# Gate and up weights of the next expert issued ahead of the down weights of the current one

## The chip, the cores and the metric

The kernel runs on one core of a Trainium2 chip. The metric is the device time of one execution in microseconds (us). Before the change it is 1476.72 us, the median of three runs (1476.27 to 1479.73 us).

## The reference, cut to what matters

One layer of a streaming encoder for 1024 prompt rows and 128 sample rows of width 1024: attention and a gated linear recurrence, an output projection, and then a mixture of 16 experts. Each row goes to two experts of one group of four. The change is in the expert stage only:

```python
for e in range(N_EXPERTS):                       # 16
    u = silu(hf @ w_e_gate[e]) * (hf @ w_e_up[e])      # 1024 -> 512
    y = y + gates[:, e:e+1] * (u @ w_e_down[e])        # 512 -> 1024
```

All values are float32. The weights of an expert are a gate, an up and a down matrix of 2 MB each.

## The kernel before, in words

The stages before the experts (conditioning, projection, mixing, output projection, routing) are not touched. The routing stage sorts the routed rows into lists of up to 128 rows that all go to the same expert, the lists of expert 0 first. The profiled execution has 27 lists (L2085 runs once for each). The routing stage also issues the loads of experts 0 and 1, before the lists are known (L1622, L1623).

The expert stage (`experts`, from L1758) walks through the lists. A matrix product in float32 is made of three in a shorter format: each operand is split in a high part (a copy by ScalarE, ACT) and the rest (a subtraction by VectorE, DVE). The weights lie in two slots by the expert's parity: `w_gu` (gate and up) and `w_dn` (down). The rest replaces the loaded weights in place. The high part of gate and up, `w_h`, has a single buffer; that of down, `w_dh`, has two.

In the step of list t, TensorE (PE) runs `hidden(t)` (48 matmuls, L1942 to L1944), `turn_x(t+1)` (8 transposes, L1927), `down(t-1)` (24 matmuls, L1958 to L1960) and `turn_u(t)` (4 transposes, L1966). So the first record of L1927 in a step marks the end of a list's hidden matmuls.

When list t is the last of its expert, ACT and DVE split the next expert's weights in this step. The order on ACT is fixed by the program: silu of list t, `keep_x(t+1)`, eight copies of gate and up (L1996), `keep_u(t)`, a wait for the down weights (L1999, L2000), four copies of them (L2006); only then comes the silu of list t+1 (L2026). DVE follows with the rests: L2085, L2048, L2055, then L2043 (the gated result of list t-1), L2081 and L2062. `hidden(t+2)` on PE waits for `u_ready` and `xl_ready`, which DVE sets with L2085 and L2048 of the next step.

The SyncE queue (SP) issues the weight loads of experts 2 to 15. For expert e it waits until the hidden matmuls of expert e-2 are done (`gu_mm`), issues gate and up (L346), waits until the down matmuls of expert e-2 are done (`dn_mm`), and issues down (L349). Then it goes on to expert e+1. The queue is in order, so a wait of one expert holds back the loads of the next. GpSimd (POOL) issues three indirect transfers for each list on its own queue: the gather of the rows (L1861), the gather of the output gates (L1866), and the addition of the finished rows to the output in memory (L1889), which waits for DVE's L2043.

Of the kernel before, what the change touches and what calls it, by code (L numbers as in the profile page):

```python
# [50 lines left out]
NE = 16  # L51
# [7 lines left out]
LISTS = 2 * NT + NE - 1  # L59
SLOTS = LISTS + 2  # L60
# [36 lines left out]
def one(t):  # L97
    return slice(t, t + 1) if isinstance(t, int) else bass.ds(t, 1)
# [239 lines left out]
    sp.dma_start(b["w_r"][:, :, :], d["w_router"].rearrange("(k p) n -> p k n", p=P)).then_inc(b["w_r_loaded"], 16)  # L338


def load_expert(sp, b, d, e, par, after_gu=None, after_dn=None):

    if after_gu:
        sp.wait_ge(*after_gu)
    for j, w in enumerate((d["w_gate"], d["w_up"])):
        sp.dma_start(b["w_gu"][:, par, j, :, :], w[one(e), :, :].rearrange("a (k p) n -> p (a k) n", p=P)).then_inc(b["gu_loaded"][par], 16)  # L346
    if after_dn:
        sp.wait_ge(*after_dn)
    sp.dma_start(b["w_dn"][:, par, :, :], d["w_down"][one(e), :, :].rearrange("a (k p) n -> p (a k) n", p=P)).then_inc(b["dn_loaded"][par], 16)  # L349

OUT_A, OUT_B, M0, M1, M2, M3, PJ0, PJ1 = range(8)
# [1214 lines left out]
def route(nc, b, d, router_bias):  # L1568
# [3 lines left out]
    with ExitStack() as ctx:  # L1572
# [3 lines left out]
        def sem(name):  # L1576
            return ctx.enter_context(nc.semaphore("q_" + name))
# [35 lines left out]
        s = {n: sem(n) for n in names}  # L1613
        block = ctx.enter_context(nc.Block())

        @block.sync
        def _(sp):
            sp.dma_start(bias[:, :], router_bias.partition_broadcast(P)).then_inc(s["bias_loaded"], 16)

            sp.sem_inc(b["gu_loaded"][1], 1)  # L1620
            sp.sem_inc(b["dn_loaded"][1], 1)
            for e in range(2):  # L1622
                load_expert(sp, b, d, e, e)  # L1623

        @block.gpsimd
        def _(pool):
# [131 lines left out]
def experts(nc, b, d):  # L1758
# [10 lines left out]
    with ExitStack() as ctx:  # L1769
# [3 lines left out]
        def sem(name):  # L1773
            return ctx.enter_context(nc.semaphore("e_" + name))
# [21 lines left out]
        s = {n: sem(n) for n in names}  # L1796
# [17 lines left out]
        def after(base, t):  # L1814
            return slice(base + t, base + t + 1) if isinstance(t, int) else bass.ds(t + base, 1)
# [16 lines left out]

        @block.sync
        def _(sp):
            def load(e, par):

                done = sp.value_load(b["list_info"][0:1, bass.ds(e + (SLOTS - 2), 1)], min_val=0, max_val=LISTS)
                load_expert(sp, b, d, e, par, (s["gu_mm"], done + 1), (s["dn_mm"], done + 1))

            with sp.Fori(1, NE // 2) as i:  # L1840
                load(i * 2, 0)
                load(i * 2 + 1, 1)
            for par in range(2):
                sp.wait_ge(gu_loaded[par], NE * 16 + par)
                sp.wait_ge(dn_loaded[par], NE // 2 * 16 + par)
# [290 lines left out]
```

## Time and profile before

| | |
|---|---|
| median of three runs | 1476.72 us |
| profiled execution | 1478.23 us |
| span of its trace | 1476.5 us |
| PE busy | 1276.9 us (86% of the span) |
| DVE busy | 771.5 us (52%) |
| ACT busy | 545.0 us (37%) |
| weight loads by L346 and L349 | 48 of 2048 KB |

The page cuts the span into 40 slices of 36.9 us. In the last fifteen, the expert stage, PE is mostly at nine tenths, and the DMA engines' share reads 7 to 9 tenths in most:

```profile
PE   5529999999999999994969973699999999969964
PEclk7759999999999999995779995799999999989988
DMA  9970000000000000005273328458667979898874
```

Each digit is the busy share of a slice in tenths; PEclk is the clock granted to TensorE, in tenths of full speed. Where PE reads 6 late in the span, PE has stood still.

### The profile page before, as it was taken

The numbers are of one execution on the slowest core, as the hardware profiler recorded it, in microseconds if no ns is written. First come the engines' busy times: TensorE is split into PE (matmuls) and PEld (weight loads), VectorE is DVE, ScalarE is ACT, GpSimd is POOL, SyncE is SP. The second block draws the span as 40 slices with busy tenths as digits, with TensorE's granted clock in tenths as the row PEclk, the third lists the DMA queues.
The fourth block names the chain that finished last, engine by engine and source line by source line (L and its number), as shares of the span: only waits on it lengthen the run. The fifth ranks groups of instructions, "written<-read, shape, count | busy, mean of one in ns | idle before, by whom it ended". The sixth has DMA issues, their size and how long they took to land. (4 is left out here: it accounts for less than half of the span.)

```text
span 1476.5 us, 21409 instructions
## 1 busy us (share of the span) xinstructions
PE 1276.9 (86%) x6661; PEld 919.6 (62%) x6662; DVE 771.5 (52%) x1187; ACT 545.0 (37%) x916; POOL 264.5 (18%) x287
## 2 busy tenths in 40 slices
PE   5529999999999999994969973699999999969964
PEld 0014666665766666564648863588888787858853
DVE  0010656466475655647244446555528665865752
ACT  0011535435253443524143330444416444644540
POOL 1000101102010110204000000233133233323313
PEclk7759999999999999995779995799999999989988
DMA  9970000000000000005273328458667979898874
GB/s 355 415 286 11 5 15 0 14 0 14 14 0 14 0 14 0 14 2 130 38 202 124 118 100 291 151 182 273 215 184 250 332 256 309 300 309 253 266 281 85
DMA packets 87921, 215.01 MB, mean 146 GB/s; under 512 B 16577, under 2 KB 20289, under 8 KB 84818
## 3 DMA queue, kind: packets, MB, share of 16 engines
q1 hardware_dynamic: 75794, 170.58, 32.3%
q0 software_dynamic: 12096, 44.05, 11.4%
q8 instruction: 16, 0.26, 0.1%
q14 instruction: 15, 0.12, 0.0%
HBM read 188.31 MB, written 26.23 MB: 145 GB/s over the span
## 5 line engine op out<-in xcount | busy, mean ns | idle before, releaser
L481 PE MATMUL psum<-w_in_sb,x_res 128*128 128x512 f32 (+1 forms) x864 | 353.2, 563 | 4.4 <-DVE x_res L471 4.4
L481 PEld LDWEIGHTS psum<-w_in_sb,x_res 128*128 128x128 f32 x864 | 160.9, 191 | 164.1 <-issue 156.8
L1942 PE MATMUL psum<-e_w_h,e_x_h 128*128 128x512 f32 x432 | 174.9, 405 | 29.5 <-DVE w_gu L2055 23.1
L1943 PE MATMUL psum<-w_gu,e_x_h 128*128 x432 | 171.8, 398 | 0.0
L1944 PE MATMUL psum<-e_w_h,e_x_l 128*128 128x512 f32 x432 | 171.6, 397 | 0.0
L2055 DVE TENSOR_TENSOR w_gu<-w_gu,e_w_h 128x1024 f32 x128 | 146.7, 1220 | 20.5 <-ACT e_w_h L1996 20.5
L1996 ACT ACTIVATE e_w_h<-w_gu 128x1024 fp32r x128 | 123.0, 1048 | 53.9 <-issue 33.0
L1889 POOL DMA_INDIRECT out<-e_work,e_to x26 | 87.6, 3371 | 302.3 <-DVE e_work L2043 302.3
L1942 PEld LDWEIGHTS psum<-e_w_h,e_x_h 128*128 128x128 f32 x432 | 83.4, 193 | 47.9 <-DVE w_gu L2055 23.6
L1944 PEld LDWEIGHTS psum<-e_w_h,e_x_l 128*128 128x128 f32 x432 | 83.3, 193 | 18.2
L1943 PEld LDWEIGHTS psum<-w_gu,e_x_h 128*128 128x128 f32 x432 | 83.4, 193 | 17.0
L1958 PE MATMUL psum<-e_w_dh,e_u_h 128*128 x216 | 86.5, 400 | 2.1 <-DVE e_u_l L2081 2.1
L1960 PE MATMUL psum<-e_w_dh,e_u_l 128*128 x216 | 84.4, 391 | 0.0
L1959 PE MATMUL psum<-w_dn,e_u_h 128*128 x216 | 84.2, 390 | 0.0
L2085 DVE TENSOR_TENSOR e_work<-e_work,psum 128x512 f32<-128x512 f32 x27 | 18.6, 687 | 125.2 <-ACT e_work L2026 123.1
L2062 DVE TENSOR_TENSOR w_dn<-w_dn,e_w_dh x64 | 74.0, 1222 | 18.9 <-ACT e_w_dh L2006 18.9
L2026 ACT ACTIVATE e_work<-psum 128x512 f32<-128x512 f32 x27 | 16.1, 597 | 173.8 <-PE psum L1944 173.8
L2006 ACT ACTIVATE e_w_dh<-w_dn x64 | 62.4, 1050 | 30.3 <-DMA w_dn<-in_w_e_down 30.3
L576 PE MATMUL psum<-q_l,k_l 64*128 64x64 f32 x896 | 68.1, 276 | 5.6 <-DVE pair L802 3.7
L576 PEld LDWEIGHTS psum<-q_l,k_l 64*128 64x128 f32 x896 | 60.0, 187 | 19.5 <-issue 11.2
L1413 PE MATMUL psum<-r_w_h,r_lhs_h 128*128 128x512 f32 x144 | 58.9, 409 | 12.7 <-DVE r_w_l L1541 12.1
L470 DVE TENSOR_TENSOR x_res<-psum,mod_a 128x1024 f32<-128x1024 f32 x10 | 12.2, 1224 | 108.6 <-PE psum L460 108.6
(393 smaller groups left out, 2055.9 us busy)
## 6 DMA issues: line engine op xcount, KB each, us to landing
w_gu<-in_w_e_gate SPq DMA_DIRECT2D x16, 2048.0 KB, 11.0
w_gu<-in_w_e_up SPq DMA_DIRECT2D x16, 2048.0 KB, 15.8
w_dn<-in_w_e_down SPq DMA_DIRECT2D x16, 2048.0 KB, 15.2
stage<-in_w_ada SPq DMA_DIRECT2D x24, 1024.0 KB, 13.2
x_res<-in_x SPq DMA_DIRECT2D x20, 512.0 KB, 3.7
w_in_sb<-in_w_in SPq DMA_DIRECT2D x5, 2048.0 KB, 19.0
out<-r_x SPq DMA_DIRECT2D x9, 512.0 KB, 2.6
h_d<-r_h SPq DMA_DIRECT2D x9, 512.0 KB, 2.9
```

What stands on the lines that cost most here:

```text
L481: last = pe.matmul(psum[:, PJ0 + j % 2, 0:n], h_t[:, k, :], b["w_in_sb"][:, k, a:a + n], start=(k == 0), stop=(k == KC - 1))
L576: last = pe.matmul(o, k_l[r, i % 2, c * P:(c + 1) * P], q_l[r, i % 2, c * HD:(c + 1) * HD], start=True, stop=True)
L1889: pool.indirect_dma_start(out=d["y"], out_offset=bass.IndirectOffsetOnAxis(ap=to_now[1 - par][:, 0:1], axis=0), in_=y_s[:, 1 - par, :], in ...
L1942: pe.matmul(psum[:, j, :], x_h[:, k, :], wh, start=(k == 0), stop=False)
L1943: pe.matmul(psum[:, j, :], x_h[:, k, :], wl, start=False, stop=False)
L1944: last = pe.matmul(psum[:, j, :], x_l[:, k, :], wh, start=False, stop=(k == KC - 1))
L1958: pe.matmul(psum[:, 5 + j, :], u_h[:, k, :], wh, start=(k == 0), stop=False)
L1959: pe.matmul(psum[:, 5 + j, :], u_h[:, k, :], wl, start=False, stop=False)
L1960: last = pe.matmul(psum[:, 5 + j, :], u_l[:, k, :], wh, start=False, stop=(k == KD - 1))
L1996: nc.scalar.activation(w_h[:, :, k, :], part(w_gu, bass.ds(e % 2, 1), k), ACT.Copy).then_inc(s["wh_ready"], 1)
L2055: dve.tensor_tensor(w.bitcast(F32R), w, w_h[:, :, k, :].bitcast(F32), ALU.subtract).then_inc(s["wl_ready"], 1)
L2062: dve.tensor_tensor(w.bitcast(F32R), w, row_of(w_dh, slot, k).bitcast(F32), ALU.subtract).then_inc(s["wdl_ready"], 1)
```

## The change

`load_expert` is cut into `load_gate_up` and `load_down`; neither waits by itself. The SP queue keeps the same two waits, with the same counts, but in another order: the gate and up loads of expert e+1 come ahead of the down load of expert e. The loads of experts 0 and 1 stay as they were, and so does everything on the other engines.

```diff
-def load_expert(sp, b, d, e, par, after_gu=None, after_dn=None):
-    if after_gu:
-        sp.wait_ge(*after_gu)
+def load_gate_up(sp, b, d, e, par):
     for j, w in enumerate((d["w_gate"], d["w_up"])):
         sp.dma_start(b["w_gu"][:, par, j, :, :], w[one(e), :, :].rearrange("a (k p) n -> p (a k) n", p=P)).then_inc(b["gu_loaded"][par], 16)
-    if after_dn:
-        sp.wait_ge(*after_dn)
+
+def load_down(sp, b, d, e, par):
     sp.dma_start(b["w_dn"][:, par, :, :], d["w_down"][one(e), :, :].rearrange("a (k p) n -> p (a k) n", p=P)).then_inc(b["dn_loaded"][par], 16)
...
-            def load(e, par):
-                done = sp.value_load(b["list_info"][0:1, bass.ds(e + (SLOTS - 2), 1)], min_val=0, max_val=LISTS)
-                load_expert(sp, b, d, e, par, (s["gu_mm"], done + 1), (s["dn_mm"], done + 1))
-            with sp.Fori(1, NE // 2) as i:
-                load(i * 2, 0)
-                load(i * 2 + 1, 1)
+            def uses_done(e):
+                return sp.value_load(b["list_info"][0:1, after(SLOTS - 2, e)], min_val=0, max_val=LISTS)
+            def gate_up(e, par):
+                sp.wait_ge(s["gu_mm"], uses_done(e) + 1)
+                load_gate_up(sp, b, d, e, par)
+            def down(e, par):
+                sp.wait_ge(s["dn_mm"], uses_done(e) + 1)
+                load_down(sp, b, d, e, par)
+            gate_up(2, 0)
+            with sp.Fori(1, NE // 2 - 1) as i:
+                gate_up(i * 2 + 1, 1)
+                down(i * 2, 0)
+                gate_up(i * 2 + 2, 0)
+                down(i * 2 + 1, 1)
+            gate_up(NE - 1, 1)
+            down(NE - 2, 0)
+            down(NE - 1, 1)
```

## Rows read from the trace of the kernel before

**Rows 1.** Windows: busy us (count) by engine, clock, DMA share, GB/s; expert stage.

```profile
925.00:1477.00 552.00, 491.92 (x2276) 406.02 (x2276) 320.01 (x304) 242.44 (x275) 170.62 (x168) 0.94 0.75 242
```

**Rows 2.** Waits, expert stage: who waited for whom, total us, times, longest us.

```profile
ACT e_w_dh L2006 <- DMA w_dn<-in_w_e_down: 30.3, 4, 8.5
...
ACT e_w_h L1996 <- DMA w_gu<-in_w_e_up: 20.9, 2, 10.5
```

**Rows 3.** Timeline, PE, L1927: start us, us, instruction, count.

```profile
1107.08 1.03 PE L1927 MATMUL psum<-ident,e_work 128*128 128x128 f32 x8
...
1124.80 1.03 PE L1927 MATMUL psum<-ident,e_work 128*128 128x128 f32 x8
...
1142.52 1.03 PE L1927 MATMUL psum<-ident,e_work 128*128 128x128 f32 x8
...
1164.31 0.93 PE L1927 MATMUL psum<-ident,e_work 128*128 128x128 f32 x7
...
1235.16 1.04 PE L1927 MATMUL psum<-ident,e_work 128*128 128x128 f32 x8
...
1254.56 0.71 PE L1927 MATMUL psum<-ident,e_work 128*128 128x128 f32 x5
...
1290.00 1.03 PE L1927 MATMUL psum<-ident,e_work 128*128 128x128 f32 x8
...
1323.28 0.93 PE L1927 MATMUL psum<-ident,e_work 128*128 128x128 f32 x7
...
1411.84 1.03 PE L1927 MATMUL psum<-ident,e_work 128*128 128x128 f32 x8
...
1444.48 1.03 PE L1927 MATMUL psum<-ident,e_work 128*128 128x128 f32 x8
```

**Rows 4.** Timeline, SP queue: issue start us, us, load.

```profile
1107.42 0.38 SPq L346 DMA_DIRECT2D w_gu<-in_w_e_gate  x1
1107.90 0.53 SPq L346 DMA_DIRECT2D w_gu<-in_w_e_up  x1
1131.34 0.37 SPq L349 DMA_DIRECT2D w_dn<-in_w_e_down  x1
1132.89 0.38 SPq L346 DMA_DIRECT2D w_gu<-in_w_e_gate  x1
```

**Rows 5.** DMA view, issues at 1107.4, 1132.9 and 1255.4: KB, us to landing.

```profile
w_gu<-in_w_e_gate SPq DMA_DIRECT2D x1, 2048.0 KB, 8.2
w_gu<-in_w_e_up SPq DMA_DIRECT2D x1, 2048.0 KB, 13.1
...
w_gu<-in_w_e_gate SPq DMA_DIRECT2D x1, 2048.0 KB, 19.5
w_gu<-in_w_e_up SPq DMA_DIRECT2D x1, 2048.0 KB, 24.4
...
w_gu<-in_w_e_up SPq DMA_DIRECT2D x1, 2048.0 KB, 16.0
```

**Rows 6.** Chain that ended last, expert stage: start us, us, its DMA pieces.

```profile
1131.34 10.77 DMA w_dn<-in_w_e_down
...
1223.98 10.05 DMA w_dn<-in_w_e_down
...
1280.60 24.90 DMA w_gu<-in_w_e_up
...
1402.44 25.77 DMA w_gu<-in_w_e_up
```

**Rows 7.** Timeline, ACT at the first late down load: idle before, releaser in brackets.

```profile
1142.48 3.91 ACT L2006 ACTIVATE e_w_dh<-w_dn  x4 [7.52 <-DMA w_dn<-in_w_e_down]
```

**Rows 8.** Timeline, POOL, L1889 in two steps that split weights.

```profile
1121.57 5.77 POOL L1889 DMA_INDIRECT out<-e_work,e_to  x1 [17.41 <-DVE e_work L2043]
...
1139.29 1.61 POOL L1889 DMA_INDIRECT out<-e_work,e_to  x1 [6.55 <-DVE e_work L2043]
```

**Rows 9.** Windows: PE after its first stall, columns as in Rows 1.

```profile
1151.70:1155.00 3.30, 3.28 (x8) 2.61 (x9) 0.86 (x2) 0.00 (x0) 1.82 (x2) 0.50 1.05 390
```

More of the change, by code:

```diff
@@ L1622, in _ @@
             for e in range(2):
-                load_expert(sp, b, d, e, e)
+                load_gate_up(sp, b, d, e, e)
+                load_down(sp, b, d, e, e)
         @block.gpsimd
```

## The prediction

> **What bounds the kernel now.** I read the page's slices first, to find the expert stage; then the windows, the waits and the chain inside it; then PE's timeline from list to list; last the SP queue's timeline with the landing of each load. In the stage PE works 492 of 552 us, at a granted clock of 0.94, while the DMA engines are busy for 0.75 of the time [rows 1]. So PE sets the pace, and what matters is where it stands still. Its starts of L1927 give the step: 1107.08 to 1124.80 and on to 1142.52 are 17.72 us each [rows 3], and all but four of the intervals from the third list on read so. The four are A, 1142.52 to 1164.31 (21.79); B, 1235.16 to 1254.56 (19.40); C, 1290.00 to 1323.28 (33.28); D, 1411.84 to 1444.48 (32.64). Over the step they cost 4.1 + 1.7 + 15.6 + 14.9 = 36.2 us. The chain shows a load ahead of each: down in A and B, up in C and D [rows 6]; the waits say the same, 30.3 us on down in four places and 20.9 us on gate and up in two [rows 2].
>
> Which list ends which expert follows from the SP queue: gate and up are issued 0.3 us after the hidden matmuls that they wait for, unless the queue is held. Read so, experts 4, 7, 9, 10, 13, 14 and 15 have one list, 2 and 3 have three, and the others two: 27. Call H(e) the end of the hidden matmuls of the last list of expert e-1, the moment at which ACT and DVE turn to the weights of e. In the rows H(4) is 1107.08 and H(5) is 1124.80.
>
> **What moves earlier.** Gate and up of e+1 need only H(e). At H(4) they go out at once, 1107.42; at H(5) they wait behind down(5), which leaves at 1131.34, and go at 1132.89, 8.1 us late [rows 3, 4]. This happens only where e-1 has a single list, that is at H(5), H(8), H(10), H(11) and H(14): five of thirteen. In the eight others gate and up already leave at H and gain nothing. In C and D (gate and up issued behind H(10) and H(14)) the up load lands 24.9 and 25.8 us after its issue, about 15 us after the H that needs it [rows 3, 6]. Issued at H with nothing in front it takes 13.1 to 16.0 us [rows 5], less than a step, so it lands in time and C and D lose their cause. A and B are caused by a late down load; they are inside the new cost below, so all 36.2 us are taken off here and the new waits are put in whole.
>
> **What moves later.** Down(e) needs only the down matmuls of e-2, done about 6.5 us after the end of the first hidden list of e-1: one step before H(e) for an expert of two lists, two steps for three. Before the change it left then and lay there in time. Now it leaves after gate and up of e+1, so never before H(e), and behind 4 MB in its queue. It costs no instruction more; SP's own issues stay under PE's work. The question is when it lands after H; call that L.
>
> Gate and up take 13.1 us from the up issue at 1107.90, so up is in 13.9 us after H(4); from the issue at 1255.38, 16.0 us, so 16.8 after H(9) [rows 3 to 5]. The eight landings read this way are 13.9 to 14.6 in three cases (H(3), H(4), H(6)) and 16.1 to 16.8 in five. A further 2 MB behind them costs 5.4 us: gate lands at 1115.6 and up at 1121.0; gate at 1152.4 and up at 1157.3, again about 5 [rows 4, 5]. With POOL's transfers beside it one load costs more: down(5) lands at 1142.1, the gate behind it 10.3 us later [rows 4 to 6], so at most 4.9 us more. POOL's addition L1889 starts 14.5 us after H(5) (1139.29) in the step where ACT waits for down, and its issue takes 1.61 us; beside DVE's L2062 it takes 5.77 [rows 8]. Its bytes move some 4 us behind that, so they meet down where it lands late. I take 1 us of the 4.9 for the early three and 2.5 for the late five. So L = 14.2 + 5.4 + 1 = 20.6 (three) and 16.5 + 5.4 + 2.5 = 24.4 (five). The bounds are 19.3 (13.9 + 5.4) and 26.8 (16.5 + 5.4 + 4.9).
>
> The Trainium skill bears on both of these. Its page GPSIMD Engine Reference, section Key points, says that GpSimd shares its SBUF interfaces with VectorE when a VectorE instruction has two SBUF inputs, as L2062 has. The 5.77 against 1.61 us agrees, and by it the change itself sends L1889's bytes into the down load, since DVE waits there; if it did not hold, the 1 and 2.5 us would fall away and the time would be about 1522. And DMA: Bandwidth & Descriptors, section Where 436 GB/s comes from, has reads from HBM bound at about 358 GB/s a core; by that 2 MB would cost 5.9 us and the estimate would be some 10 us higher. The trace differs: 5.4 us are 388 GB/s, and it decides.
>
> **What a late down load costs.** ACT reaches its wait for down 10.1 us after H, and in A it stands there 7.52 us [rows 7]. All that follows on ACT and DVE is queued behind it: four copies, four rests, then silu, L2085 and L2048 of the next list, for which the hidden matmuls after the next wait. Down(e) itself is not needed on PE for more than a step. From landing to the L1927 behind those hidden matmuls it is 1164.31 - 1142.11 = 22.2 us in A and 1254.56 - 1234.03 = 20.5 in B [rows 3, 6]. A contains 3.3 us at half clock [rows 9], B, whose gap is shorter, none; the new gaps are longer than A's, so 22.2. Without a wait the same two steps take 35.4, so a late landing costs L + 22.2 - 35.4 = L - 13.2: 7.4 us in three cases, 11.2 in five, sum 78.2.
>
> The five H behind a single-list expert follow one step behind another H. There the loads queue: a whole set of three takes 5.4 x 3 + 4.9 = 21.1 us, against the 17.7 that the step grants, so each of H(5), H(8), H(10), H(14) adds 3.4, sum 13.6. H(11) is third in a row; the queue has run dry by then, so it has an L of its own: 24.4 + 22.2 after H(11), of which the step of H(10) already holds 38.8; it adds 7.8. Down(15) has no gate and up in front, leaves 6.5 us after H(15) and lands near 16.5, under the 16.6 of B by which little is lost. New cost 78.2 + 13.6 + 7.8 = 99.6; net 99.6 - 36.2 = 63.4 us. On the profiled execution that is 1478.2 + 63.4 = 1541.6; the median lies 1.5 below it, so 1540.
>
> **The bounds.** With no meeting of POOL's bytes and half the clock's price (L of 19.6 and 21.9, cost L - 14.1) the eight give 55.5, the followers some 9: net +28, 1505. The lowest that rows allow is L = 19.3 at every place and B's 20.5 throughout: 4.4 x 9, net +3, 1480. With all 4.9 us everywhere (24.5 and 26.8) the eight give 101.9, the followers 24: net +90, 1566.
>
> **The rivals.** (1) The other side: down is loaded well before it is wanted and lands under PE's work even now, so that only the 36 us go: 1441. For it speaks that PE wants down(e) more than a step later. Against it, A and B show the wait holding up ACT's whole row with landings of only 17.3 and 16.6 us after H. It decides at L = 15; my lowest is 19.3. Chance 5%. (2) A late down load, but at the floor of both prices, 1478 to 1500, because the new gaps drain the queue and take POOL's bytes out of its way: 8%. (3) The DMA engines become the bound: POOL's transfers and three loads need more than the set's 21.1 us, and each delay shifts POOL's bursts onto the next set, or the clock stays low for longer than 3.3 us after a gap of 8 us: 1566 and above, 10%. (4) My case, 1500 to 1566: 75%; the last 2% for no measurable difference. That the change does not do what it says can be left aside: the two waits and their counts stay, and only the order in the queue differs.
>
> **How the numbers follow.** Predicted 1540, range 1500 to 1566. About 0.3% (4 us) can be told from no change: faster 0.05, same 0.03, slower 0.92.
>
> **What would show it.** Waits: ACT L2006 on the down load in some thirteen places instead of four, about 10.5 us each for the early and 14 for the others, 170 us in all; the wait of L1996 on gate and up gone, and with it the two 33 us intervals. Intervals of L1927: behind each H one of 17.7 and one of 25 to 29 us. The SP queue: down issued 1 to 2 us after up. The stage's clock below 0.94. I am wrong if down lands within 15 us of H, if PE does not stand still although ACT waits, or if a load in the same queue does not wait for those ahead of it.

## The result and the profile after

The changed kernel takes 1515.32 us (median of six runs, 1512.51 to 1517.43) against 1478.89 us for the kernel before, measured beside it. The ratio is 1.0247 (95% interval 1.0231 to 1.0263): slower, as forecast, by 36 us where 63 were forecast. The profiled execution took 1515.84 us (span 1514.1), 37.6 more than the one of before.

The windows view of the expert stage, and the longest load waits in it, answer to [rows 1, 2]:

```profile
925.00:1514.00 589.00, 509.34 (x2280) 415.85 (x2278) 320.84 (x307) 241.15 (x275) 127.76 (x168) 0.93 0.71 229
```

```profile
ACT e_w_dh L2019 <- DMA w_dn<-in_w_e_down: 125.5, 14, 10.8
DVE w_dn L2075 <- ACT e_w_dh L2019: 79.3, 13, 8.0
ACT e_w_h L2009 <- DMA w_gu<-in_w_e_up: 32.1, 1, 32.1
...
PE psum L1955 <- DVE w_gu L2068: 16.0, 6, 2.7
```

The stage has grown by 37 us. In 17 of them PE is busy, with nearly the same number of instructions (2280 against 2276): behind most of the new stalls its granted clock reads 0.50 for some microseconds. ACT waits for a down load in 14 places instead of four. The wait for gate and up that is left, 32.1 us, is the one ahead of the first list, which in the trace of before is put down to "issue"; the two of [rows 2] are gone. One hand-over, to expert 2, shows the whole mechanism. First the SP queue, then the landings of these three loads, then ACT, then POOL (answering to [rows 4, 5, 7, 8]):

```profile
1002.17 0.38 SPq L344 DMA_DIRECT2D w_gu<-in_w_e_gate  x1
1002.65 0.54 SPq L344 DMA_DIRECT2D w_gu<-in_w_e_up  x1
1004.12 3.27 SPq L349 DMA_DIRECT2D w_dn<-in_w_e_down  x1
```

```profile
w_gu<-in_w_e_gate SPq DMA_DIRECT2D x1, 2048.0 KB, 8.5
w_gu<-in_w_e_up SPq DMA_DIRECT2D x1, 2048.0 KB, 13.4
...
w_dn<-in_w_e_down SPq DMA_DIRECT2D x1, 2048.0 KB, 18.3
```

```profile
1022.79 2.01 ACT L2019 ACTIVATE e_w_dh<-w_dn  x2 [10.80 <-DMA w_dn<-in_w_e_down]
```

```profile
1016.31 1.61 POOL L1902 DMA_INDIRECT out<-e_work,e_to  x1 [17.73 <-DVE e_work L2056]
```

The chain that ended last now runs through these loads:

```profile
1004.12 18.30 DMA w_dn<-in_w_e_down
```

PE's starts of L1940 (the line of [rows 3], now L1940) show what follows:

```profile
1001.83 1.03 PE L1940 MATMUL psum<-ident,e_work 128*128 128x128 f32 x8
...
1019.55 1.03 PE L1940 MATMUL psum<-ident,e_work 128*128 128x128 f32 x8
...
1044.72 1.04 PE L1940 MATMUL psum<-ident,e_work 128*128 128x128 f32 x8
...
1062.41 1.03 PE L1940 MATMUL psum<-ident,e_work 128*128 128x128 f32 x8
```

H(2) is 1001.83, and down lands at 1022.4, which is 20.6 us later. The next interval is still 17.72 us. The one after it is 25.17, because silu and the rests of that step stood behind the wait on ACT and DVE. All thirteen hand-overs, read in the same way (L from landing less H; the cost is what the later interval has over 17.72):

| hand-over | L, us | cost, us |
|---|---|---|
| H(2), H(3), H(4) | 20.6, 19.3, 19.7 | 7.5, 7.3, 8.4 |
| H(6), H(7), H(9) | 19.3, 19.2, 19.3 | 5.9, 8.0, 7.2 |
| H(12), H(13) | 20.0, 19.3 | 6.5, 7.7 |
| H(5), H(8), H(10), H(11), H(14) | 23.5, 24.1, 23.9, 22.1, 23.7 | 0.4, 1.2, 3.2, 5.5, 2.7 |

The first eight sum to 58.4 us, the five behind a single-list expert to 13.1: 71.5 in all. The 36.2 us of before have gone, which leaves 35.3; the rest of the 37.6 lies ahead of the third list (1.1) and behind the last (1.4).

### The profile page after: what moved, and what is told of

Same layout as the page of the kernel before. It is cut to its first block and busy times, and to the rows that moved or that the text cites. A ratio compares the mean times of both kernels' runs of the same rounds, so it can differ in the third digit from the quotient of the medians.

```text
span 1514.1 us, 21465 instructions
## 1 busy us (share of the span) xinstructions
PE 1293.8 (85%) x6661; PEld 929.1 (61%) x6662; DVE 770.7 (51%) x1187; ACT 543.8 (36%) x916; POOL 221.8 (15%) x287
## 5 line engine op out<-in xcount | busy, mean ns | idle before, releaser
L1955 PE MATMUL psum<-e_w_h,e_x_h 128*128 128x512 f32 x432 | 180.1, 417 | 28.5 <-DVE w_gu L2068 16.0
L1956 PE MATMUL psum<-w_gu,e_x_h 128*128 x432 | 176.0, 407 | 0.0
L1957 PE MATMUL psum<-e_w_h,e_x_l 128*128 128x512 f32 x432 | 175.7, 407 | 0.0
L2009 ACT ACTIVATE e_w_h<-w_gu 128x1024 fp32r x128 | 123.0, 1048 | 32.1 <-DMA w_gu<-in_w_e_up 32.1
L2019 ACT ACTIVATE e_w_dh<-w_dn x64 | 62.5, 1048 | 125.5 <-DMA w_dn<-in_w_e_down 125.5
L1902 POOL DMA_INDIRECT out<-e_work,e_to x26 | 50.2, 1933 | 378.8 <-DVE e_work L2056 378.8
L1956 PEld LDWEIGHTS psum<-w_gu,e_x_h 128*128 128x128 f32 x432 | 86.5, 200 | 18.0
L1957 PEld LDWEIGHTS psum<-e_w_h,e_x_l 128*128 128x128 f32 x432 | 85.8, 199 | 18.9
L2098 DVE TENSOR_TENSOR e_work<-e_work,psum 128x512 f32<-128x512 f32 x27 | 18.6, 688 | 138.1 <-ACT e_work L2039 133.9
L2039 ACT ACTIVATE e_work<-psum 128x512 f32<-128x512 f32 x27 | 15.9, 587 | 148.1 <-PE psum L1957 148.1
## 6 DMA issues: line engine op xcount, KB each, us to landing
w_gu<-in_w_e_up SPq DMA_DIRECT2D x16, 2048.0 KB, 13.9
```

The lines of the kernel that those rows point to most:

```text
L1955: pe.matmul(psum[:, j, :], x_h[:, k, :], wh, start=(k == 0), stop=False)
L1956: pe.matmul(psum[:, j, :], x_h[:, k, :], wl, start=False, stop=False)
L1957: last = pe.matmul(psum[:, j, :], x_l[:, k, :], wh, start=False, stop=(k == KC - 1))
L2009: nc.scalar.activation(w_h[:, :, k, :], part(w_gu, bass.ds(e % 2, 1), k), ACT.Copy).then_inc(s["wh_ready"], 1)
L2019: nc.scalar.activation(row_of(w_dh, slot, k), row_of(w_dn, slot, k), ACT.Copy).then_inc(s["wdh_ready"], 1)
```

## The experiments

H, L and the cost mean what they did above. The kernel before took 1477.4 to 1478.1 us beside these runs.

**e1: the changed kernel, the split of down one step later.**

```diff
                 with act.If(e > 0):
                     weights_in(e)
                     split_gu(e, range(KC))
-                    keep_u(t)
-                    split_dn(e, t)
-                with act.Else():
-                    keep_u(t)
+                keep_u(t)
+                if not is_first(t):
+                    now = act.value_load(b["list_info"][0:1, after(SPLIT - 1, t)], min_val=0, max_val=NE - 1)
+                    with act.If(now > 0):
+                        split_dn(now, t)
```

VectorE is changed in the same way: `split_dn(now, nth_now)`, with the count of one list earlier.

> The changed kernel, with the split of an expert's down weights moved on ACT and DVE from the step of the last list before that expert to the step of its own first list, same place in the step. The wait for the down load then comes 17.7 us later after the hand-over. Theory (the late down load costs time only because ACT's and DVE's rows are queued behind it): down lands some 20 us after H, the wait comes at about 28, so all thirteen new gaps (71.7 us between the 27 list starts) go and the 36.2 us of before do not come back: 1441 to 1450 us, below the kernel before. Rival (three loads packed together at H crowd the gathers or keep PE's clock down by themselves): the gaps stay in good part, 1490 to 1515 us.

Measured: 1444.91 us, ratio 0.9771 (0.9741 to 0.9801), in the theory's range. The SP queue is that of the changed kernel, and at the eight hand-overs down lands 19.2 to 23.1 us after H. Yet every interval of PE from the third list to the end is 17.69 to 17.72 us. The windows view of the stage, and the waits on down:

```profile
925.00:1442.00 517.00, 485.50 (x2276) 402.42 (x2276) 320.63 (x301) 243.70 (x275) 149.72 (x168) 0.97 0.79 259
```

```profile
ACT e_w_dh L2019 <- DMA w_dn<-in_w_e_down: 4.1, 1, 4.1
```

The DMA share is higher than in the changed kernel and the clock too. The rival, that the packed loads cost by themselves, is refuted: the whole cost ran through the place of one wait, and of the split behind it, in the rows of ACT and DVE. This version beats both kernels.

**e2: the kernel before, with the same move.** The edit is that of e1 on the old order of loads.

> The kernel before the change, old order of loads, with the same move of the down split as in e1. Theory: only the two small gaps whose chain shows a late down load go (4.1 and 1.7 us); the two of 15 us, which wait for gate and up queued behind down, stay: 1471 to 1475 us. If e1 gains and this one does not, the order of loads is worth its 30 us once the wait is moved. Rival (the move by itself is what gains, whatever the order): 1441 to 1450 us here as well.

Measured: 1465.95 us, ratio 0.9908 (0.9875 to 0.9940), lower than the theory's 1471 to 1475 and far from the rival's 1441 to 1450. A and B are gone; C and D are there but have shrunk from 33.3 and 32.6 to 28.1 and 27.5 us. The up load behind H(10) lands 28.3 us after it, not 33.2 [rows 6]: POOL's transfers fall elsewhere when DVE does not split down in that step. Together e1 and e2 show that the new order of loads is worth 21 us once the wait stands later, and costs 36 where it stands now.

**e3: half of gate and up.** Left out: the second half of the gate and up weights of experts 2 to 15.

```diff
+    half = slice(0, KC // 2) if not isinstance(e, int) or e >= 2 else slice(0, KC)
     for j, w in enumerate((d["w_gate"], d["w_up"])):
-        sp.dma_start(b["w_gu"][:, par, j, :, :], w[one(e), :, :].rearrange("a (k p) n -> p (a k) n", p=P)).then_inc(b["gu_loaded"][par], 16)
+        sp.dma_start(b["w_gu"][:, par, j, half, :], w[one(e), :, :].rearrange("a (k p) n -> p (a k) n", p=P)[:, half, :]).then_inc(b["gu_loaded"][par], 16)
```

> The changed kernel, loading for experts 2 to 15 only half of gate and of up (the first four of eight row blocks; the others keep stale weights). All else is the same, the splits and matmuls too. Down still leaves at H and never before, but behind 2 MB instead of 4. Theory (cost = L + 22 to 23 - 35.4, L from the bytes ahead of it): L falls from 19.6 to about 14.2, ACT waits 4 us instead of 9.5, and the cost at the eight hand-overs falls to between 0 and 1.5 us each: 1443 to 1455 us. Rival (what costs is that down leaves at H at all): most of the cost stays, over 1490 us.

Measured: 1462.05 us, ratio 0.9896 (0.9858 to 0.9934). The rival is refuted, but the theory's range is missed by 7 us. At the eight hand-overs it held exactly: L 13.4 to 14.2, ACT waits some 4 us each, and PE's intervals are 17.72. I had not seen the others: behind a single-list expert down leaves only 6.5 us after H and lands at 17.7 to 18.6, which costs 3.3, 2.9, 7.3 and 6.6 us at four intervals. The waits of this kernel:

```profile
ACT e_w_dh L2020 <- DMA w_dn<-in_w_e_down: 69.5, 14, 8.5
```

So 69.5 us of waiting stand for 20 us of lost time, and 125.5 in the changed kernel for 71.5. A wait up to L = 14.2, the longest of the eight, was free. The first cost, 3.3 us, is seen at L = 18.1 (H(5)), so my estimate is that the wait is free up to about 14.8.

**e4: down held back until H, but ahead in the queue.**

```diff
+            def down_at_hand_over(e, par):
+                held, done = uses_done(e + 1) + 1, uses_done(e) + 1
+                sp.wait_ge(s["gu_mm"], held)
+                sp.sem_inc(s["waits_alone"], 1)
+                sp.wait_ge(s["dn_mm"], done)
+                load_down(sp, b, d, e, par)
...
+                down_at_hand_over(i * 2, 0)
                 gate_up(i * 2 + 1, 1)
-                down(i * 2, 0)
+                down_at_hand_over(i * 2 + 1, 1)
                 gate_up(i * 2 + 2, 0)
-                down(i * 2 + 1, 1)
```

> The old order, down of e ahead of gate and up of e+1, but down held back until H(e) by an added wait on the hidden matmuls of e-1. So down leaves as late as in the changed kernel, only not behind 4 MB. Theory: L is 8.5 to 11 where e-1 has several lists, under the 10.1 us at which ACT asks for it, so the eight hand-overs cost nothing from down; up lands 19 us after H, in time except perhaps by a microsecond or two where a single-list expert follows; the four gaps of before stay: 1477 to 1488 us. Rival (leaving at H is the cost, not the queue ahead): 1505 us or more.

Measured: 1478.99 us, ratio 1.0012 (0.9995 to 1.0029): no difference from the kernel before, as the theory had it. Down lands 7.8 to 8.2 us after H at the eight hand-overs and nothing waits for it; the four gaps of before are there, 36.3 us in sum. The landing of the load issued 0.5 us after H(2):

```profile
w_dn<-in_w_e_down SPq DMA_DIRECT2D x1, 2048.0 KB, 7.7
```

At the eight hand-overs leaving late is harmless by itself. What costs there is leaving late and behind 4 MB.

**e5: the new order only behind a single-list expert.**

```diff
+            def both(e, par):
+                lists = sp.value_load(b["list_info"][0:1, after(ENDS - 1, e)], min_val=0, max_val=LISTS) - uses_done(e)
+                with sp.If(lists > 1):
+                    down(e, par)
+                    gate_up(e + 1, 1 - par)
+                with sp.Else():
+                    gate_up(e + 1, 1 - par)
+                    down(e, par)
...
-                gate_up(i * 2 + 1, 1)
-                down(i * 2, 0)
-                gate_up(i * 2 + 2, 0)
-                down(i * 2 + 1, 1)
+                both(i * 2, 0)
+                both(i * 2 + 1, 1)
```

> The changed kernel, in the new order only where expert e-1 has a single list (the SP queue compares two list counts at each hand-over); elsewhere down of e first, as before. So down leaves a step or more before H at eight hand-overs and lies behind 4 MB at five. Theory: no cost at the eight; at H(5), H(8), H(10) and H(14) down lands near 19.5 and costs some 7 us each, at H(11) with a queue still full 4 to 6; the two gaps of 15 us stay away. From the 1441 to 1445 us of a stage without gaps: 1472 to 1482 us, the kernel before within its noise. Rival (the cost sits mostly at the hand-overs where the loads already queue, the five): close to the changed kernel, over 1495 us.

Measured: 1514.07 us, ratio 1.0246 (1.0222 to 1.0270). My forecast missed by over 30 us, and the time is that of the rival. But the reason that I had given for the rival, that the cost sits at these five, does not hold for the changed kernel, where they cost only 13.1 us. The eight cost nothing here; four intervals cost 16.8, 16.9, 18.9 and 19.2, 71.8 in all. Around H(5), at 1125.45, the queue, the landing of the down load, ACT, and PE's next two starts:

```profile
1125.80 0.38 SPq L344 DMA_DIRECT2D w_gu<-in_w_e_gate  x1
1126.27 0.53 SPq L344 DMA_DIRECT2D w_gu<-in_w_e_up  x1
1132.14 4.17 SPq L349 DMA_DIRECT2D w_dn<-in_w_e_down  x1
```

```profile
w_dn<-in_w_e_down SPq DMA_DIRECT2D x1, 2048.0 KB, 23.5
```

```profile
1155.97 2.00 ACT L2025 ACTIVATE e_w_dh<-w_dn  x2 [20.36 <-DMA w_dn<-in_w_e_down]
```

```profile
1143.17 1.03 PE L1946 MATMUL psum<-ident,e_work 128*128 128x128 f32 x8
...
1177.71 1.03 PE L1946 MATMUL psum<-ident,e_work 128*128 128x128 f32 x8
```

L is 30.2 us, and PE comes 22.1 us behind the landing, as in A [rows 3, 6]. The price law holds; L was wrong. POOL's timeline shows two bursts within these 30 us:

```profile
1122.21 5.77 POOL L1908 DMA_INDIRECT out<-e_work,e_to  x1 [17.43 <-DVE e_work L2062]
...
1128.98 1.84 POOL L1885 DMA_INDIRECT e_work<-out_gate_d,e_kind  x1 [0.80 <-POOL e_kind L1871]
...
1131.94 1.11 POOL L1880 DMA_INDIRECT e_work<-h_d,e_from  x1 [0.81 <-POOL e_from L1871]
...
1139.94 1.61 POOL L1908 DMA_INDIRECT out<-e_work,e_to  x1 [6.55 <-DVE e_work L2062]
```

What POOL's queue moved between H(5) and the landing of down, by the DMA view, first in e5 and then in the changed kernel:

```profile
q0 software_dynamic: 864, 3.15, 34.5%
```

```profile
q0 software_dynamic: 446, 1.63, 25.2%
```

That is 3.15 MB against 1.63. In the changed kernel DVE waits for down in the step before H(5). L1902 is issued there in 1.61 us, so that burst starts earlier, and the next L1902 comes only 21.3 us behind H(5), since the stall holds back DVE's L2056. One burst meets the loads, and L is 23.5. In e5 that step does not wait. The issue takes 5.77 us beside DVE's down split, so the gathers are issued 3.5 and 6.5 us after H(5), not 0.6 ahead of it and 1.4 after, and the second burst starts 14.5 us behind H(5). Most of the difference arises there: up lands 20.0 us after H(5) against 18.5, and down 10.2 us behind up against 5.0.

e1 shows that no stall is needed for the shorter L. Nothing waits for down there at H(4), but DVE's down split stands one step later; the first issue takes 1.61 us and the second 5.76, POOL moves 1.78 MB, and L is 22.9 at H(5) and 22.9 to 23.4 at H(8), H(10) and H(14). So at these hand-overs L goes with where POOL's bursts fall, and a wait of DVE is one thing that moves them. At H(5) this is 6.7 of the 16.4 us between the costs of the two kernels; the other 10 are there because the changed kernel stands still in that step for H(4) already. The costs of hand-overs do not add up.

**e6: down between gate and up.** The order in the loop is gate of e+1, down of e, up of e+1, with the same two waits.

```diff
-                gate_up(i * 2 + 1, 1)
-                down(i * 2, 0)
-                gate_up(i * 2 + 2, 0)
-                down(i * 2 + 1, 1)
+                gate(i * 2 + 1, 1)
+                down(i * 2, 0)
+                load_one(i * 2 + 1, 1, 1)
+                gate(i * 2 + 2, 0)
+                down(i * 2 + 1, 1)
+                load_one(i * 2 + 2, 0, 1)
```

> The changed kernel with down of e between gate and up of e+1: 2 MB ahead of it instead of 4, and all the loads whole. Theory: L is about 14 at the eight hand-overs as with the halved loads, so no cost there; behind a single-list expert down leaves at 6.5, with the gate load already under way, and lands near 14 to 15 too, so nothing there either; up lands 19.5 to 24 us after H and is wanted 19.8 after it where a single-list expert follows, which may cost 0 to 4 us in up to seven places: 1443 to 1462 us. Rival (with all 6 MB to move at H the queue is the limit in any order): 1490 us or more.

Measured: 1464.18 us, ratio 0.9902 (0.9873 to 0.9930), 2 us over the theory's range and far from the rival's. L is 13.9 to 14.3 at the eight, which cost nothing. The loss is again behind single-list experts: down lands there at 17.0 to 20.0 and up at 25 to 28.5, which costs 5.0, 2.2, 6.8 and 8.9 us.

**e7 and e8: fewer of POOL's bytes.** Both cut the gather of the output gates from 1024 to 128 columns and leave the others out. e7 does so on e5, e8 on the changed kernel.

```diff
-            def fetch_gates(par):
+            def fetch_gates(par, n=D):
                 alone()
-                pool.indirect_dma_start(out=gate_g[:, par, :], out_offset=None, in_=d["out_gate"],
+                pool.indirect_dma_start(out=gate_g[:, par, 0:n], out_offset=None, in_=d["out_gate"].rearrange("t (a n) -> (t a) n", n=n),
...
-                    fetch_gates(1 - par)
+                    fetch_gates(1 - par, 128)
```

> The kernel of e5 with POOL's gather of the output gates cut from 1024 to 128 columns a row in all steps but the first two fetches (the gates used are then not the right ones; the number of instructions is the same). In e5 down landed 29 to 31 us after H at five hand-overs, and two bursts of POOL's three transfers lie within that time. Theory (their bytes share the 16 DMA engines with the three loads, and make 30 out of 19.5): some 0.9 MB less in that time, 2.4 to 4.8 us at the rates seen (388 and 190 GB/s), five times: 1490 to 1503 us. Rival (the loads queue behind one another for another reason, POOL's share is small): within 4 us of e5, 1510 to 1518 us.

Measured: 1506.88 us, between the theory's range (1490 to 1503) and the rival's (1510 to 1518): 7 us less than e5, where the theory had 11 to 24. L at the five falls from 30.2, 30.1, 30.9, 29.1 and 30.3 to 28.1, 28.7, 27.9, 26.1 and 28.5. So POOL's bytes do lengthen L, by 2.3 us in the mean for some 0.9 MB. The other two transfers were not cut, so that they make up the rest of the 10 us is argued from the timeline, not shown.

> The changed kernel with the same cut of the output gates' gather as in e7. At the eight hand-overs behind an expert of several lists down lands 19.2 to 20.6 us after H with no POOL bytes beside the loads. Theory: these eight, 58 of the 72 us of gaps, stay as they are, and only the five others gain a little: 1506 to 1514 us. Rival (POOL's bytes matter there as well, as the prediction had it with 1 and 2.5 us): 10 us less or more, under 1505 us.

Measured: 1512.36 us, ratio 1.0232 (1.0203 to 1.0262), in the theory's range. L at the eight stays between 19.2 and 21.5, and their gaps sum to 59.2 us against 58.4. The gates' gather is no part of the cost there. For POOL's addition this run shows nothing, as it was not cut: from 14 us after H to the landing POOL's queue moves 0.2 to 0.3 MB at seven of the eight in the changed kernel, and 0.5 MB at H(2), where L is the longest.

## Why the prediction was right, and where its size was off

- **What moves earlier.** Right. Gate and up go out 0.2 to 0.3 us after H at all thirteen hand-overs, and C and D are gone. e2 keeps them and e1 does not.
- **What moves later.** Right in kind: down is issued 2.1 to 2.3 us after H at the eight hand-overs and lands behind 4 MB. e3, e4 and e6 show that at these it takes both, the late issue and 4 MB ahead.
- **The size of L: the term that failed.** The prediction had 20.6 us at three hand-overs and 24.4 at five; measured are 19.3 to 19.7 and 19.2 to 20.6. For the five I took the up load's landing of 16.5 us after H from the trace of before and added 2.5 us for POOL. (At H(13) that trace gives 15.9 us, not 16.1 or more.) But in that trace the old down load, issued one step earlier, was still in flight at those H: issued at 989.58, it lands at 1006.2, 5.4 us after H(2). The change takes that load away from there. In the changed kernel up lands 14.2 us after H(2).

  The old down load is not the whole of it. In the first 8 us after H(2) POOL's queue moved 1.07 MB in the kernel before and 0.01 MB in the changed one, although its gathers were issued 6.4 and 4.4 us ahead of H(2) in both. And e2, with the old order, has both cases: behind H(2) down is in ahead of H, POOL moves 0.53 MB, and up lands at 14.0 us; behind H(6) down is in 0.3 us after H, but POOL moves 1.32 MB, and up lands at 16.0. So I had read in the landings of before the transfers that were then in flight, down and gathers, and the change takes both away from there; how the 2.3 us split between them is not shown. Of POOL's 1 and 2.5 us beside the down load little occurred: down lands 5.0 to 5.3 us behind up at seven of the eight, and 6.4 at H(2).

  With 5.4 us for down behind an up load at 14, L is the 19.3 that I gave as the lower bound. This term overstated the gaps by 27 us (1.2 us at three, 4.7 at five); the price below takes off 7 and the followers add 8, together the 28 between 99.6 and 71.5.
- **The price, L - 13.2.** Nearly right, and too low: from landing to the later list's end it is 21.9 to 24.2 us at the eight, 23.1 in the mean, against A's 22.2. That is 7 us more in all. It is 23.4 to 24.2 at H(4), H(7), H(9) and H(13), where the delayed step must itself split the next expert and PE then waits 2.7 us for the first rests. At H(3), with 23.4, that reason does not apply.

  The clock is the other difference. I gave the new gaps A's price, with its 3.3 us at half clock [rows 9], although I had said that they are longer than A's. Behind H(6) and H(12), with the shortest gaps of the eight, the clock is at 0.50 for some 3.4 us too, and the price is 22.1 and 21.9; behind the six others it is so for some 6.8 us. The two lines are of the step behind H(4) and of that behind H(6); the clock stands before the DMA share:

```profile
1151.90:1158.60 6.70, 5.61 (x13) 4.44 (x14) 6.70 (x7) 4.34 (x6) 0.00 (x0) 0.50 1.05 392
1213.10:1216.40 3.30, 2.71 (x6) 2.15 (x7) 1.40 (x2) 0.00 (x0) 1.65 (x2) 0.51 0.00 0
```

  That would fit H(3) as well, but H(2) has 6.8 us at half clock and a price of 22.3. How much of the 7 us is the clock's and how much the next split's is not shown.
- **The five behind single-list experts.** Forecast 21.4 us, measured 13.1. That they add little because their predecessor has already stalled was right; e5 shows how much this depends on it: 72 us when the predecessors do not stall and POOL's bursts fall elsewhere. I had treated the costs as separate terms.
- **The rivals.** That down is hidden behind PE's work was wrong because of the wait's place alone: with the wait one step later, e1 takes 1444.9 us, near the 1441 that this rival named. The floor of both prices (1478 to 1500) and the DMA engines as a bound (1566 and above) did not come: e1 moves the same bytes in 33 us less than the kernel before. One of the third rival's conditions did come, a clock that stays low for longer than 3.3 us behind the new gaps, but without the price that it named.
- **The Trainium skill** (GPSIMD Engine Reference, section Key points) has GpSimd share SBUF interfaces with a VectorE instruction that has two SBUF inputs. The traces agree: L1902 takes 1.61 us where DVE waits, and L1908 5.77 us beside the down split in e5. But what I drew from it, an earlier burst that meets the down load at once, came to 0.2 to 0.5 MB at the eight hand-overs and shows in L at H(2) at most; its main effect lies one hand-over later, with the other sign.

## What to carry to other kernels

Before a load is moved back in a queue, look up in the program's order at which point its consumer engine asks for it. The matmul that needs it may be far off, but an in-order engine that waits for it holds back all that stands behind. Move the wait together with the load: here the new order costs 36 us with the wait where it was, and gives 33 us with the wait one step later. And when a landing time is read from the old trace, check which transfers were in flight beside it, and whether the change moves those.

## What the runs showed that I had not expected

- A 2 MB load issued at the same point of the step takes 16.6 us in the kernel before and 8.5 us in e2, although only the down split moved, by a step. POOL's transfers moved with it: its queue carries 2.56 MB during the first of these loads and 0.26 MB during the second. The two landings, of the down load of expert 2, in before and in e2:

```profile
w_dn<-in_w_e_down SPq DMA_DIRECT2D x1, 2048.0 KB, 16.6
```

```profile
w_dn<-in_w_e_down SPq DMA_DIRECT2D x1, 2048.0 KB, 8.5
```

- POOL's busy time in the stage fell from 170.62 us [rows 1] to 127.76, as L1902 was issued more often beside a waiting DVE. That this saved time of the kernel is not shown.
